# Five edits to one long kernel: the norms' root on columns, the pool layer's copies on ScalarE, an earlier context load, and work moved ahead of three waits

## The chip, the cores and the metric

The kernel runs on one core of one Trainium2 chip. The metric is device time in microseconds for one execution, as the median of several runs. The engines of the core are TensorE (PE, with its weight loads as PEld), VectorE (DVE), ScalarE (ACT), GpSimd (POOL) and SyncE (SP), which mostly issues DMAs.

## The reference, cut to what matters

Two transformer-like blocks follow each other on 512 tokens of 1024 features, all in float32. Every sub-layer begins with the same norm over the features:

```python
def rmsnorm(x, g):
    xf = x.astype(jnp.float32)
    y = xf * lax.rsqrt(jnp.mean(xf * xf, axis=-1, keepdims=True) + EPS)
    return (y * g.astype(jnp.float32)).astype(x.dtype)
```

The first block has four layers: mixers Hyena, windowed attention, pooling and Hyena, each followed by a SwiGLU feed-forward, so eight norms. The pooling mixer takes, for four groups of 256 features, the mean over windows of 3, 5, 9 and 17 tokens, subtracts the input, multiplies each group by a 256x256 matrix, adds a bias and scales. The second block takes a condition vector and a context of 256 tokens. Its two norms are modulated, `norm(x) * (1 + scale) + shift`, with scale and shift from the condition. The first modulated norm is applied to the context too. Then come a bidirectional gated delta rule over eight heads in chunks (it needs the inverse of a unit triangular matrix of each chunk), a latent attention over eight heads, a gated merge of both, and a squared-ReLU MLP.

## The kernel before, in words

All activations lie transposed, feature on partition and token on the free axis. `x` and `xn` are 8 tiles of 128x512. Each engine has one hand-written program, and the engines meet through semaphores. `schedule` gives the stages; each engine has a handler for each stage (`norm`, `hyena`, `attention`, `pool_mixer`, `ffn`, `mod`, `modulate`, `decays`, `gdn`, `mla`, `merge`, `mlp`) and runs them in order. All weights come as one stream of blocks through a ring of four slots. SP issues the loads, and a slot comes free when a named semaphore has a named value. Large products are made in three float32r passes from a high and a low part (L880 to L882 in `split_product`, L891 to L893 in `split_pair`); ACT makes the high part of the weights (L1748) and POOL the low part (L774). PSUM has eight banks: four for `acc` tiles and four for `aux` tiles; in the delta rule they are dealt out as three tables of tiles (`A_AT`, `P_AT`, `R_AT`).

**The norm.** ACT squares the eight tiles of `x` into `xn`, the last one once the last residual tile is there (L1764). DVE folds seven of them into `xn[:, 0]` as they come (L2336). PE multiplies a 128x128 matrix of ones with the folded tile (L867) and with the last square (L870), which leaves the sum over features in every row of one bank. ACT takes the root over 128x512 (L1791), DVE the reciprocal over 128x512 into `rstd` (L2322 in `norm`, L2626 in `modulate`), and then DVE makes the eight tiles of `xn` from `x`, the gain and `rstd` (L2327, or L2628 and L2629). Ahead of a feed-forward each tile is split into a high part on ACT (L1755) and a low part on DVE (L2307); PE starts on the first tile when both are there and goes on tile by tile. There are ten such norms, eight in `norm` and two in `modulate`. The context has its own (L1196 on PE, L2006 on ACT, L2641 on DVE), which the change leaves as it is.

**The pool layer.** DVE does all of it but the products. After the norm it clears two buffers (L2568, L2569), makes the bias column (L2570), and for each of the eight tiles copies `xn` into the padded buffer `xp` (L2575), doubles windows by adding shifted copies (L2578, one to four times), adds, multiplies and subtracts (L2581 to L2583), and adds the bias to `x` (L2584). Then the residual follows. PE's fifth product needs the bank of the first, so it waits for the first residual (L2349).

**The context load.** In stage `mod`, after the last feed-forward, ACT waits for its last product, issues two DMAs (tables, L1994, and the context into `work`, L1995), waits for both, and only then goes into `modulate`, whose first work are the last two squares of the norm.

**The delta rule.** `gdn` on PE runs eleven steps `t`. A step projects head `t` (`proj`, L1314, in pieces of two or four products, set between other work), forms the products of head `t-1` (`products`), and runs the recurrence of head `t-2` (`lows`, `fills`, `flips` on 32- and 64-wide blocks, then `tr`, `sn`, `ks`, `outs`), each of which waits for ACT or DVE to have emptied the one before. The triangular blocks of 32 are solved by POOL; SP writes them out, waits, and reads them back in another layout; PE waits for them on `blocks_in` ahead of the first `lows` (L1352). At t = 9 and after, the pieces named `q`, `z`, `k` and so on stand for the latent attention's down projections (`TAIL`, L1295); there `q` is a tile of sums whose bank ACT and DVE empty after the last solved blocks are written out.

**The latent attention.** `mla` on DVE ends its set-up with `maxima(0)`, the row maxima of the first unit of scores, after the last pair's `mod_sums`, `heads` and `mod_out`. ACT's `exps(0)` needs them, and it is what empties the two banks that PE's `scores(2)` (L1611, L1612) writes. PE makes `scores(0)` and `scores(1)` first of all, then the last pair's broadcast rows (L1553), a rotation (L1602) and two groups of modulation sums (L1185).

## Time and profile before

| | |
|---|---|
| median of 3 runs | 4485.65 us (4485.53 to 4496.6) |
| the profiled execution's own time | 4489.94 us |
| its span, first to last instruction | 4488.1 us |
| PE busy (matmul), DVE, POOL, ACT | 93%, 47%, 32%, 27% of the span |
| mean granted TensorE clock | 0.956 of full speed |

PE bounds nearly everything, but the busy share of a matmul counts its pipeline too, and it counts a matmul at half the clock as work. A reader looks for stretches in which PE stands still or has its clock halved. In the timeline, a row gives start, length, engine, line, operation, tiles and shapes, how many instructions were merged, and in brackets the idle time of the engine before it with what ended it. A float32 matmul is recorded as two. The granted clock in the windows view is 1.00 at full speed (2.4 GHz) and 0.50 at half (1.2 GHz).

### The profile page before, as it was taken

The page shows a single profiled execution, that of the slowest core. Times are in us where ns is not written, and L with a number is a line of the kernel's source. Part 1 is how long each engine was busy: PE and PEld are TensorE (multiplying, and loading weights), DVE is VectorE, ACT ScalarE, POOL GpSimd, SP SyncE. Part 2 cuts the span into 40 slices and gives each one's busy share as a digit, 9 for nine tenths or more (in the row PEclk, how much of TensorE's full clock was granted, in tenths as well). Part 3 has the DMA queues.
Part 4 walks back from the last instruction along what each step waited for, and adds up shares of the span by engine and source line. Part 5 has one row for each costly group of instructions (what it writes and reads, how often), then busy time and mean ns, then how long its engine had stood idle before and what let it go on. Part 6 is the DMA issues. An engine that isn't in the chain of part 4 may idle for free.

```text
span 4488.1 us, 47580 instructions
## 1 busy us (share of the span) xinstructions
PE 4152.2 (93%) x18926; PEld 3071.3 (68%) x18926; DVE 2123.1 (47%) x3109; ACT 1223.2 (27%) x1709; POOL 1444.5 (32%) x834
## 2 busy tenths in 40 slices
PE   7999999899999599989999998979998999998999
PEld 5656788556788378877557886656666665684887
DVE  6567323365413641375763334456664347404322
ACT  3322222134222121233233222322222224422221
POOL 3311344200344144434023442266564000241443
PEclk9999999999999899999999998989999879999999
DMA  6200232210232123221002221221112112221232
GB/s 179 75 18 21 110 102 88 104 47 29 98 114 83 61 97 115 82 78 63 29 29 103 98 95 60 69 57 33 56 34 57 58 67 66 68 98 64 86 104 78
DMA packets 96910, 333.71 MB, mean 74 GB/s; under 512 B 44337, under 2 KB 47537, under 8 KB 67889
## 3 DMA queue, kind: packets, MB, share of 16 engines
q1 hardware_dynamic: 87968, 311.85, 20.5%
q10 hardware_dynamic: 8720, 18.82, 1.7%
q8 instruction: 151, 2.47, 0.2%
q14 instruction: 71, 0.57, 0.0%
HBM read 317.53 MB, written 13.11 MB: 74 GB/s over the span
## 4 chain that ended last, share of the span: by engine, by line
PE 79%; DVE 14%; POOL 2%; ACT 2%; issue 1%; DMA 1%; SPq 0%; DVEq 0%; ACTq 0%; POOLq 0%
PE bank L880 16%; PE bank L881 16%; PE bank L882 16%; PE bank L1314 5%; PE bank L859 5%; PE bank L1082 3%; PE bank L1032 1%; PE bank L1056 1%; PE bank L1612 1%; PE bank L1611 1%; PE bank L1633 1%; PE bank L1543 1%; DVE xn L2327 1%; POOL tab L761 1%; POOL tab L759 1%
## 5 line engine op out<-in xcount | busy, mean ns | idle before, releaser
L774 POOL TENSOR_TENSOR w_lo<-ring,w_hi 128x2048 fp32r<-128x2048 f32 (+2 forms) x200 | 775.3, 3877 | 1532.7 <-ACT w_hi L1748 1532.7
L880 PE MATMUL bank<-x_hi,w_hi 128*128 128x512 f32 x1584 | 618.3, 390 | 9.7 <-POOL w_lo L774 9.7
L881 PE MATMUL bank<-x_lo,w_hi 128*128 128x512 f32 x1584 | 617.0, 389 | 0.0
L882 PE MATMUL bank<-x_hi,w_lo 128*128 128x512 f32 x1584 | 616.9, 389 | 0.0
L1748 ACT ACTIVATE w_hi<-ring 128x2048 fp32r<-128x2048 f32 (+2 forms) x200 | 322.0, 1610 | 866.9 <-PE bank L882 865.9
L880 PE MATMUL bank<-h_hi,w_hi 128*128 128x512 f32 x960 | 373.9, 389 | 0.4
L881 PE MATMUL bank<-h_lo,w_hi 128*128 128x512 f32 x960 | 373.5, 389 | 0.0
L882 PE MATMUL bank<-h_hi,w_lo 128*128 128x512 f32 x960 | 373.4, 389 | 0.0
L880 PEld LDWEIGHTS bank<-x_hi,w_hi 128*128 128x128 f32 x1584 | 297.7, 188 | 73.4 <-POOL w_lo L774 11.8
L882 PEld LDWEIGHTS bank<-x_hi,w_lo 128*128 128x128 f32 x1584 | 297.8, 188 | 61.9
L881 PEld LDWEIGHTS bank<-x_lo,w_hi 128*128 128x128 f32 x1584 | 297.8, 188 | 61.6
L2363 DVE TENSOR_TENSOR xn<-bank,xn 128x512 f32<-128x512 f32 x88 | 60.8, 691 | 589.0 <-PE bank L882 570.0
L1314 PE MATMUL bank<-xn,ring 128*128 128x512 f32 x496 | 240.0, 621 | 1.4 <-DVE work L2671 1.4
L1082 PE MATMUL bank<-work,tab 128*128 128x512 f32 x512 | 228.0, 603 | 12.5 <-ACT work L1886 11.5
L787 POOL TENSOR_TENSOR ring_r<-ring,merge_hi 128x2048 fp32r<-128x2048 f32 x16 | 73.3, 4584 | 506.8 <-ACT merge_hi L2213 506.8
L2353 DVE TENSOR_TENSOR x<-bank,x 128x512 f32<-128x512 f32 x72 | 49.8, 692 | 393.8 <-PE bank L882 347.3
L880 PEld LDWEIGHTS bank<-h_hi,w_hi 128*128 128x128 f32 x960 | 180.2, 188 | 39.3 <-DVE h_lo L2313 2.1
L882 PEld LDWEIGHTS bank<-h_hi,w_lo 128*128 128x128 f32 x960 | 180.2, 188 | 37.4
L881 PEld LDWEIGHTS bank<-h_lo,w_hi 128*128 128x128 f32 x960 | 180.2, 188 | 37.3
L1082 PEld LDWEIGHTS bank<-work,tab 128*128 128x128 f32 x512 | 97.8, 193 | 133.4 <-issue 126.9
L810 POOL TENSOR_TENSOR work<-work,ring 128x1024 f32<-128x1024 f32 x32 | 77.0, 2429 | 266.4 <-ACT work L1855 266.4
L761 POOL TENSOR_TENSOR tab<-tab 56x31 f32<-56x31 f32 (+15 forms) x248 | 150.7, 608 | 19.4
(457 smaller groups left out, 7394.4 us busy)
## 6 DMA issues: line engine op xcount, KB each, us to landing
ring<-stream SPq DMA_DIRECT2D x212, 1024.0 KB, 4.8
ring<-stream SPq DMA_DIRECT2D x64, 704.0 KB, 4.1
ring<-stream SPq DMA_DIRECT2D x36, 512.0 KB, 3.6
xn<-first_mods SPq DMA_DIRECT2D x8, 1024.0 KB, 6.9
ring<-stream SPq DMA_DIRECT2D x4, 1088.0 KB, 5.0
bias_rows<-work ACTq DMA_DIRECT2D x1, 4096.0 KB, 46.3
work<-bias_rows ACTq DMA_DIRECT2D x1, 3072.0 KB, 11.3
tab<-tabs ACTq DMA_DIRECT2D x1, 2624.0 KB, 16.7
```

The lines of the kernel that those rows point to most:

```text
L761: solve(tt(W[:, 0:i, i:SUB], W[:, 0:i, i:SUB], part, ALU.subtract))
L774: nc.gpsimd.tensor_tensor(w_lo[:, j % 2, 0:cols], ring[:, k % RING, 0:cols], w_hi[:, j % 2, 0:cols], ALU.subtract).then_inc(wlo_set, 1)
L787: nc.gpsimd.tensor_tensor(ring_r[:, w, 0:2 * DT * P], ring[:, w, 0:2 * DT * P], merge_whi[j % 2][:], ALU.subtract).then_inc(wlo_set, 1)
L810: nc.gpsimd.tensor_tensor(pair, pair, decay[:, pq:pq + 1, :].broadcast_to([P, 2, 512]), ALU.mult).then_inc(filt_set, 1)
L859: ins = mm(b[:], w[:, at + k, :], rhs[k] if isinstance(rhs, list) else rhs[:, k, :], start=(k == 0), stop=(k == kt - 1))
L880: mm(b[:], hi[:, at + k, :], rhs_hi, start=(k == 0), stop=False)
L881: mm(b[:], hi[:, at + k, :], rhs_lo[:, k, :], start=False, stop=False)
L882: ins = mm(b[:], lo[:, at + k, :], rhs_hi, start=False, stop=(k == kt - 1))
L1082: ins = mm(b[:], fwd[kind][:, p, q, ft * P:(ft + 1) * P], source(kind)[:, 2 * p + q, :], start=(q == 0), stop=(q == 1))
L1314: ins = mm(b[:, 0:TC] if ctx else b[:], w[:, at + k, :], src[:, k, :], start=(k == 0), stop=(k == DT - 1))
L1748: signal(go(w_hi[:, j % 2, 0:cols], ring[:, k % RING, 0:cols], ACT.Copy), whi_set)
L2363: drain(tt_(h_tmp[:, f % 2, :], bank(t)[:], gate_tmp[:, f % 2, :], ALU.mult), t)
```

## The change

Five edits, in the order of the schedule.

1. **Root on columns.** PE uses the squares as the stationary operand and a column of ones as the moving one, in four matmuls for the folded tile and four for the last square. This gives 128x4 sums twice. DVE copies the first and adds the second into `rstd_col`, ACT takes the root of 128x4, DVE the reciprocal of 128x4, and PE spreads it with four matmuls (a broadcast column as stationary operand, the identity as moving) over a second `aux` bank. DVE's eight products read that bank in the place of `rstd`. A small memset after them frees the bank.
2. **Pool layer.** `xp` has two halves. ACT copies each `xn` tile into one and adds the bias to `x`. DVE's memsets and the bias column go into that layer's norm, ahead of the wait for the sums.
3. **Context load.** ACT issues both DMAs at the start of the last feed-forward. The context lies in `tab` and no longer in `work`. The wait stands in `modulate`, ahead of the context's squares.
4. **Projections ahead of `blocks_in`.** At t = 2 and t = 9 PE does the second half of `z` and all of `k` ahead of the wait. The later calls for these pieces do nothing.
5. **`maxima(0)`** on DVE stands between the last pair's `norm_columns` and its `mod_sums`.

```diff
         one_col = small_t[:, 7:8]
+        rstd_col = small_t[:, 28:32]

...
         hc, o_gdn, gates = carve((DT, TC), (DT, T), (8, UNITS * GH))
-        ctx_raw = carve((1, HOLD), (DT, TC))[1]
+        ctx_raw = tab[:, NTAB2:NTAB2 + DT * TC].rearrange("p (a b) -> p a b", a=DT)

...
         KSEQ, KCTX = slice(TC, MK), slice(0, TC)
-        (xp, sums, dpool) = carve((1, T + 2 * PAD), (2, T + 2 * PAD), (DT, T))
+        (xp, sums, dpool) = carve((2, T + 2 * PAD), (2, T + 2 * PAD), (DT, T))

...
                 pe.wait_ge(folded_set, n["fold"])
-                mm(b[:], ones[:], xn[:, 0, :], start=True, stop=False)
+                for c in range(NB):
+                    mm(b[:, c:c + 1], xn[:, 0, P * c:P * (c + 1)], ones[:, 0:1], start=True, stop=True)
                 n["sq"] += DT
                 pe.wait_ge(squares_set, n["sq"])
-                mm(b[:], ones[:], xn[:, DT - 1, :], start=False, stop=True).then_inc(aux_full, 1)
+                for c in range(NB):
+                    ins = mm(b[:, NB + c:NB + c + 1], xn[:, DT - 1, P * c:P * (c + 1)], ones[:, 0:1], start=True, stop=True)
+                ins.then_inc(aux_full, 1)
+                b = open_aux()
+                pe.wait_ge(rstd_set, n["fold"])
+                for c in range(NB):
+                    ins = mm(b[:, P * c:P * (c + 1)], rstd_col[:, c:c + 1].broadcast_to([P, P]), ident[:], start=True, stop=True)
+                ins.then_inc(aux_full, 1)
                 n["xn"] += DT
...
                 def proj(name, h, lo, hi):
-                    if name == "q" and h == 0:
+                    if name == "q" and h == 0 or hi <= made.get((name, h), 0):
                         return
+                    made[name, h] = hi
                     if h >= GH:
...
                     products(mid, 5)
+                    if t in (2, GH + 1):
+                        proj("z", new, 4, 8)
+                        proj("k", new, 0, 8)
                     if live:
...
                 step(go(small_t[:, 26:27], one_col, ACT.Sqrt))
-                t = full(aux, aux_full)
-                signal(go(rstd, bank(t, aux=True)[:], ACT.Sqrt, bias=eps_col, scale=1.0 / D), root_set)
+                t = aux.take()
+                aux.take()
+                act.wait_ge(aux_drained[aux.place(t)], aux.turn(t) + 1)
+                signal(go(rstd_col, rstd_col, ACT.Sqrt, bias=eps_col, scale=1.0 / D), root_set)
                 if split_target(gain) == "hyena":
...
                 aux.n += 2
+                if layer == DEPTH - 1:
+                    act.dma_start(tab[:, 0:NTAB2], tabs2).then_inc(tabs2_in, 16)
+                    act.dma_start(ctx_raw, ctx_in.rearrange("(k p) t -> p k t", p=P)).then_inc(tabs2_in, 16)
                 ends.clear()
...
             def pool_mixer(s):
+                act.wait_ge(pads_set, 2)
+                for m in range(DT):
+                    act.wait_ge(xn_set, n["xn"] + m + 1)
+                    if m >= 2:
+                        act.wait_ge(pooled, m - 1)
+                    signal(go(xp[:, m % 2, PAD:PAD + T], xn[:, m, :], ACT.Copy), xp_set)
+                    signal(go(x[:, m, :], x[:, m, :], ACT.Identity, bias=bs_col[:, m:m + 1]), biased)
                 n["xn"] += DT
                 acc.n += DT

             def mod(_):
-                act.wait_ge(acc_full, acc.n)
-                act.dma_start(tab[:, 0:NTAB2], tabs2).then_inc(tabs2_in, 16)
-                act.dma_start(ctx_raw, ctx_in.rearrange("(k p) t -> p k t", p=P)).then_inc(tabs2_in, 16)
-                act.wait_ge(tabs2_in, 32)
+                pass

             def modulate(which):
                 norm(None, ("mlp", 0) if which else None)
                 n["xn"] += DT
                 if which == 0:
+                    act.wait_ge(tabs2_in, 32)
                     for k in range(DT):
...
                         fold(k)
-                t = aux.take()
-                n["root"] += 1
-                dve.wait_ge(root_set, n["root"])
-                drain(nc.vector.reciprocal(rstd, rstd), t, True)
+                if gain == ("norm_mix", 2 * DT):
+                    nc.vector.memset(sums[:], 0.0)
+                    signal(nc.vector.memset(xp[:], 0.0), pads_set)
+                    signal(tt_(bs_col, V("pl_b", 0, DT), V("pl_scale", 0, DT), ALU.mult), pads_set)
+                t, rows = rstd_rows()
                 n["xn"] += DT
                 target = split_target(gain)
                 to = (x_hi_h, xn_r) if target == "hyena" else (x_hi, x_lo)
                 for k in range(DT):
-                    signal(stt(xn[:, k, :], x[:, k, :], V(gain[0], gain[1] + k), rstd, ALU.mult, ALU.mult),
+                    signal(stt(xn[:, k, :], x[:, k, :], V(gain[0], gain[1] + k), rows, ALU.mult, ALU.mult),
                            plain_set if target else xn_set)
                     if target and k:
                         low(k - 1, *to)
+                rows_read(t)
                 if target:
...
                     n["sq"] += DT
+
+            def rstd_rows():
+                t = full(aux, aux_full)
+                b = bank(t, True)
+                step(nc.vector.tensor_copy(rstd_col, b[:, 0:NB]))
+                ins = tt_(rstd_col, b[:, NB:2 * NB], rstd_col, ALU.add)
+                drain(ins, t, True)
+                n["root"] += 1
+                dve.wait_ge(root_set, n["root"])
+                signal(nc.vector.reciprocal(rstd_col, rstd_col), rstd_set)
+                t = full(aux, aux_full)
+                return t, bank(t, True)[:]
+
+            def rows_read(t):
+                which = aux_drained[t % BANKS]
+                nc.vector.memset(small_t[:, 25:26], 0.0).then_inc(which, 1)
+                dve.wait_ge(which, t // BANKS + 1)

...
                 inv_count = ring[:, blk.place(k), 0:4 * T].rearrange("p (a b) -> p a b", a=4)
-                nc.vector.memset(sums[:], 0.0)
-                step(nc.vector.memset(xp[:], 0.0))
-                step(tt_(bs_col, V("pl_b", 0, DT), V("pl_scale", 0, DT), ALU.mult))
                 W = T + 2 * PAD
                 for m in range(DT):
                     g = m // 2
                     r = POOL_R[g]
-                    step(nc.vector.tensor_copy(xp[:, 0, PAD:PAD + T], xn[:, m, :]))
-                    src, w, side = xp[:, 0, :], 1, 0
+                    dve.wait_ge(xp_set, m + 1)
+                    src, w, side = xp[:, m % 2, :], 1, 0
                     while w < 2 * r:
                         step(tt_(sums[:, side, 0:W - w], src[:, 0:W - w], src[:, w:W], ALU.add))
                         src, w, side = sums[:, side, :], 2 * w, 1 - side
                     dst = sums[:, side, 0:T]
-                    step(tt_(dst, src[:, PAD - r:PAD - r + T], xp[:, 0, PAD + r:PAD + r + T], ALU.add))
+                    step(tt_(dst, src[:, PAD - r:PAD - r + T], xp[:, m % 2, PAD + r:PAD + r + T], ALU.add))
                     step(tt_(dst, dst, inv_count[:, g, :], ALU.mult))
                     signal(tt_(dpool[:, m, :], dst, xn[:, m, :], ALU.subtract), pooled)
-                    step(ts_(x[:, m, :], x[:, m, :], bs_col[:, m:m + 1], None, ALU.add))
                 blk.take()
+                dve.wait_ge(biased, DT)
                 residual(scale_name="pl_scale")
...
                     step(tt_(gm[:, c, :], gm[:, c, :], gain, ALU.mult))
-                t = aux.take()
-                n["root"] += 1
-                dve.wait_ge(root_set, n["root"])
-                drain(nc.vector.reciprocal(rstd, rstd), t, True)
+                t, rows = rstd_rows()
                 for k in range(DT):
-                    step(stt(xn[:, k, :], x[:, k, :], gm[:, 0, k:k + 1], rstd, ALU.mult, ALU.mult))
+                    step(stt(xn[:, k, :], x[:, k, :], gm[:, 0, k:k + 1], rows, ALU.mult, ALU.mult))
                     signal(ts_(xn[:, k, :], xn[:, k, :], modv[:, shift + k, 0:1], None, ALU.add), plain_set if which else xn_set)
                     if which and k:
                         low(k - 1)
+                rows_read(t)
                 if which:
...
                     norm_columns(p)
+                    if p == PAIRS - 1:
+                        maxima(0)
                     mod_sums(2 * p + 1)
                     heads(p)
                     mod_out(2 * p)
                     mod_out(2 * p + 1)
-                maxima(0)
                 for k in range(MLA_UNITS):
```

Left out: the declarations of four semaphores, the counts of `aux` tiles, which go up by one for each norm on SP and POOL, and the dictionary `made`.

## Rows read from the trace of the kernel before

**Rows 1.** The page, part 4: the chain that ended last, by engine.
```profile
PE 79%; DVE 14%; POOL 2%; ACT 2%; issue 1%; DMA 1%; SPq 0%; DVEq 0%; ACTq 0%; POOLq 0%
```

**Rows 2.** The waits view of TensorE: line, releaser, us in total, times, longest.
```profile
PE bank L867 <- DVE xn L2336: 38.6, 10, 15.8
```

**Rows 3.** Timeline of one norm: start us, us, instruction, [idle before, releaser].
```profile
472.98 0.69 DVE L2336 TENSOR_TENSOR xn<-xn 128x512 f32<-128x512 f32 x1
473.81 1.10 PE L867 MATMUL bank<-xn,ones 128*128 128x512 f32 x2 [1.73 <-DVE xn L2336]
474.75 1.02 PE L870 MATMUL bank<-xn,ones 128*128 128x512 f32 x2
476.66 3.35 DVE L2322 RECIPROCAL rstd_t<-rstd_t 128x512 f32<-128x512 f32 x1 [2.99 <-ACT rstd_t L1791]
480.05 1.54 DVE L2327 SCALAR_TENSOR_TENSOR xn<-x,vec,rstd_t 128x512 f32<-128x512 f32 x2
```

**Rows 4.** Timeline, three stretches: column sums, small operations and broadcasts.
```profile
2855.23 2.29 PE L1412 MATMUL bank<-ones,work 128*128 128x1 f32 x20
2861.37 2.50 PE L1423 MATMUL bank<-ident,tab 128*128 128x128 f32 x20 [0.31 <-DVE tab L2887]
2862.63 0.69 DVE L2895 TENSOR_TENSOR work<-work,bank 128x512 f32<-128x512 f32 x1 [1.32 <-PE bank L1423]
...
3441.32 0.18 DVE L2884 RECIPROCAL tab<-tab 128x4 f32<-128x4 f32 x1
...
3658.35 0.17 DVE L2930 SCALAR_TENSOR_TENSOR tab<-bank,tab 128x8 f32<-128x8 f32 x1 [15.89 <-PE bank L1543]
3658.81 0.22 ACT L2159 ACTIVATE tab<-tab 128x20 f32<-128x20 f32 x1 [9.71 <-DVE tab L2932]
```

**Rows 5.** Timeline of the pool layer: the memsets and the first tile.
```profile
1515.86 0.94 DVE L2568 MEMSET work<- 128x1056 f32 x1 [0.38 <-DVE xn L2327]
1516.86 0.50 DVE L2569 MEMSET work<- 128x528 f32 x1
...
1517.59 0.43 DVE L2575 COPY work<-xn 128x512 f32<-128x512 f32 x1
...
1520.97 0.49 DVE L2584 TENSOR_SCALAR x<-x,small_t 128x512 f32<-128x512 f32 x1
```

**Rows 6.** Timeline from the last feed-forward's end into the modulated norm.
```profile
2767.49 0.69 DVE L2353 TENSOR_TENSOR x<-bank,x 128x512 f32<-128x512 f32 x1 [6.06 <-PE bank L882]
...
2774.98 1.29 ACT L1764 ACTIVATE xn<-x 128x512 f32<-128x512 f32 x2 [19.72 <-DMA work<-ctx_in]
...
2784.57 0.75 DVE L2628 SCALAR_TENSOR_TENSOR xn<-x,gm,rstd_t 128x512 f32<-128x512 f32 x1
```

**Rows 7.** Timeline of the delta rule; last, the windows view of L1314 alone.
```profile
2948.09 2.20 PE L1352 MATMUL bank<-work 32*32 32x32 f32 x48 [17.13 <-DMA work<-solved_n]
2956.76 1.38 ACT L2101 ACTIVATE work<-bank 32x192 f32<-32x192 f32 x4 [6.04 <-PE bank L1366]
...
3022.60 1.40 PE L1352 MATMUL bank<-work 32*32 32x32 f32 x48
...
3461.15 2.20 PE L1352 MATMUL bank<-work 32*32 32x32 f32 x48 [6.76 <-DMA work<-solved_n]
...
2948.00:2969.30 21.30, 13.34 (x24) 4.57 (x24) 0.85 0.34 114
```

**Rows 8.** Timeline, then windows: PE, PEld, DVE, ACT, POOL busy, PEclk, DMA.
```profile
3680.41 1.15 DVE L2957 TENSOR_REDUCE tab<-bank 128x1 f32<-128x512 f32 x2
...
3684.18 2.04 PE L1611 MATMUL bank<-work 128*128 128x512 f32 x2 [6.63 <-ACT tab L2165]
...
3676.00:3680.00 4.00, 1.32 (x9) 0.94 (x8) 3.78 (x7) 0.00 (x0) 0.00 (x0) 1.00 0.00 0
...
3700.00:3702.00 2.00, 2.00 (x11) 2.00 (x11) 0.00 (x0) 1.69 (x5) 0.00 (x0) 0.50 0.00 0
...
2906.40:2908.40 2.00, 2.00 (x5) 0.99 (x6) 1.96 (x2) 1.55 (x2) 1.84 (x3) 0.58 0.00 0
```

More of the change, by code:

```diff
@@ L597, in norm @@
             def norm(_):
-                n["aux"] += 1
+                n["aux"] += 2
                 n["xn"] += DT
@@ L634, in modulate @@
             def modulate(which):
-                n["aux"] += 1 if which else 2
+                n["aux"] += 2 if which else 3
             def decays(_):
@@ L822, in _ @@
             nothing = count(0)
-            run({"norm": count(1), "hyena": hyena,
+            run({"norm": count(2), "hyena": hyena,
                  "attention": passes(12 + 16 * 5, 88), "pool": passes(0, DT), "ffn": split("ffn", FT + 2 * DT), "mod": nothing,
-                 "modulate": lambda which: n.update(aux=n["aux"] + (1 if which else 2)), "decays": count(2),
+                 "modulate": lambda which: n.update(aux=n["aux"] + (2 if which else 3)), "decays": count(2),
                  "gdn": gdn, "mla": nothing, "merge": merge,
@@ L1257, in gdn @@
                 until = TB2("until").rearrange("p (d i) -> p d i", d=2)
-                head_w, opened = {(0, 0): first_w[0]}, {}
+                head_w, opened, made = {(0, 0): first_w[0]}, {}, {}
                 def a_tile(*name):
```

4 lines of the change are left out of this document (added).

## The prediction

> **What bounds the kernel now.** I read the chain that ended last first: it is 79% TensorE and 14% VectorE [rows 1]. So most of the span is matmuls that this change doesn't touch, and what can be won lies where PE stands still with DVE, or a DMA, in its place. The waits view says where: the longest sum is the one ahead of the norm's sum of squares, 38.6 us in ten waits with one of 15.8 [rows 2]. The timeline of those places then gives the chain step by step [rows 3, 5, 6], and of the three waits that the last two edits address [rows 7, 8]. The reader is to see there single-engine chains, with nothing beside them, so a microsecond off the chain is a microsecond off the time, unless something else is late next.
>
> **Norm, ten times.** Now: the last fold ends at 472.98 + 0.69 = 473.67; two products with ones end at 474.75 + 1.02 = 475.77, ACT's root takes until 476.66, DVE's reciprocal over 512 columns 3.35, and the first product with the gain begins at 480.05 [rows 3]. That is 6.38 us. After: PE starts 0.14 later as now [rows 3]; eight column matmuls are 16 records, at 2.29 for 20 [rows 4] 1.85; on DVE a copy and an addition at 0.17 each, the root 0.22, the reciprocal of 128x4 0.18 [rows 4], 0.74 together; four hops between engines and one gap at about 0.1, 0.5; and the broadcast, from the start of the first matmul to DVE's first read, 2862.63 - 2861.37 = 1.26 [rows 4]. Sum 0.14 + 1.85 + 0.74 + 0.5 + 1.26 = 4.49, a gain of 1.9 each. The reciprocal was nearly all of it. Everything behind (x_hi, x_lo, the second block's high weights on ACT and low on POOL) starts from DVE's first products and moves with them, so nothing else becomes late. The memset that frees the bank is of the order of 0.1 and stands behind all eight products; only the last low part waits for it, and PE, which restarts at half clock, is then behind DVE. The unknown is the clock at the broadcast. PE does little from the last dense matmul on, and columns count as little: after a group of 20 the clock stood at 0.58 [rows 8]. If it has fallen by then, the four matmuls and their latency take up to twice 1.26, about 1.0 more. That gives 0.9 to 1.9 a norm; I take the fall in 4 cases of 10, so 1.5. Nine norms are 13.5 (8 to 17); the tenth is below. The clock at the restart of the dense work is half in both versions, so no gain is counted for it.
>
> The Trainium skill, page VectorE: DVE Perf Modes, section on the TRN2 errata, speaks against this edit: operations on SBUF pay a fixed cost each, and it advises tiles of 512 elements or more, so one wide operation should be better than several of four columns. It gives about 150 cycles at 0.96 GHz, by which the three small DVE operations would cost an estimated 0.47 us against 0.52 by the rows; the sum would be the same within 1 us for all ten norms. The rule holds for copies, not against a reciprocal that costs 3.35 for 512 columns and 0.18 for four [rows 3, 4].
>
> **Pool layer.** From each of eight tiles DVE loses a copy of 0.43 and a bias of 0.49 [rows 5] with a gap of 0.03 each: 7.8. Ahead of them go two memsets, 0.94 and 0.50, a small multiplication and the gaps, 1.7 [rows 5], less 0.1 for the new memset. Together 9.5. ACT does the same on its own time: it has the place of one tile (at least 2.9 us: four additions or multiplications at 0.7) for about 1.4 of work, and idles there now. The memsets (the second one is twice as long now) are some 2.1 us while PE makes its column sums, 2.0: hidden, or 0.1 late. Without ACT's cover each tile would wait about 0.8. Range 8.5 to 9.7.
>
> **Context load.** ACT's two last squares are made at 2774.98, after 19.72 idle and released by the DMA, though the last residual ended at 2767.49 + 0.69 = 2768.18 [rows 6]. Without it the last square and fold follow at once, and the fold ends at 2768.9, as it does 0.7 after the residual in other norms [rows 3]. With the new chain the first modulated product begins at 2768.9 + 4.5 = 2773.4 where it now begins at 2784.57 [rows 6]: 11.2. This holds the old chain's sums at half clock, too, which now come at full. Less 0.4 for the broadcast's clock: 10.8 (10 to 11.3). DVE's four small operations for the gain are done during the sums. The two issues on ACT at the start of the last feed-forward cost under 1 us, ahead of work of ACT that waits for PE. The DMAs are 1.9 MB on queues that take a 1 MB block in 4.8 us (the page's part 6) while the ring is blocks ahead: nothing, or a few microseconds once if a block is late.
>
> **Projections ahead of the blocks.** At t = 2 PE waits 17.13 and at t = 9 6.76 [rows 7]. The pieces moved ahead are 24 records of L1314, 13.34 in the stretch that follows, partly at half clock; 10.3 at full. So at t = 2 they fit into the wait. But they were the filler: between `lows` and the first `ks` PE waits six times for ACT or DVE to empty a bank (the longest, four copies, 1.38 [rows 7]), and these round trips of 0.5 to 1.5 us, 3 to 9 in all, now lie bare. At full clock t = 2 gains some 6, and is capped anyway: blocks of the next head are there not much before 3016, and its `lows` start at 3022.60 [rows 7], so 6.7 is the most. But the stretch is then all small matmuls at a clock that the wait has halved, and I expect it to stay at 1.2 GHz until the next dense product: 4 us lost on the small ones, 2 on the dense ones behind. That leaves 0.5 to 1, between -1 and 6.5. At t = 9 the pieces take longer than the wait (3.4, then a wait for the bank of the sums, then 6.9), so `lows` begin at about 3465 and not at 3461.15 [rows 7]; 3.5 gained at full clock, -1.5 if the clock falls in the small ones. I take 1.5 for both together (-3 to 10).
>
> **Maxima.** `scores(2)` waits 6.63 until 3684.18 for ACT's exponentials [rows 8], which wait for DVE's first maxima at 3680.41 [rows 8]. Moved, these come when `scores(0)` is done, some 15 us earlier, and DVE's modulation sums (4 us) behind them are still ready before the broadcast rows. So the whole 6.6 goes. More follows. The clock was 1.00 at 3676 to 3680, and it is 0.50 up to 3702 [rows 8]: the wait halves it, and PE's 17.6 us of work from 3684.2 on run at 1.2 GHz. At 2.4 GHz they take half, 8.8; DVE's second maxima and probabilities then come about 2 too late for the first transposes and give 1 to 2 of it back. Bounds 6.6 and 14; I take 12, as the loop behind it holds the full clock.
>
> The Trainium skill, page TensorE: Matmul & The Clock Gate, section HAM oscillation, says that idle gaps throttle the array again and the work behind each gap starts cold. Here the trace agrees: 1.00 before the wait, 0.50 behind it.
>
> **Sum.** 13.5 + 10.8 + 9.5 + 1.5 + 12 = 47.3. The profiled execution took 4489.94 (span 4488.1), so it would become 4442.6; it lies 4.3 over the median of the runs, which becomes 4485.65 - 47.3 = 4438.
>
> **Rivals.** (a) The gains come short: the broadcast at half clock in every norm (9 x 0.9 = 8.1), 10.3 for the modulated norm, 9 for the pool layer, -3 for the projections, since their filler is gone, and 6.6 for the maxima: 31, 4455. For it speaks that PE's activity is thin in each of these places. (b) The clock is kind: 17 + 11.2 + 9.6 + 10 + 14 = 62, 4424. For it speak small matmuls of 128 columns elsewhere at full clock; against it the 32-wide blocks. (c) Slower: the one-column matmuls of the norms hold the clock down in the dense work behind them. One such group was followed by 0.58 in the next window [rows 8]. If each of nine norms left PE at half clock for 20 us more than now, that costs 10 each: 90 - 47 = 43 slower, 4528. It decides from 47.3 x 2 / 9 = 10.5 us more per norm. Against it: the loss after that group was a matter of 3 to 4 us, which is also what a restart costs now. (d) The change doesn't do what it says: the steps between engines in norm and pool layer take 0.5 and not 0.1, and the norms (13.5) and half of the pool layer (5) bring nothing: 29, 4457, much as (a).
>
> **Chances.** Forecast (39 to 56 gained, 4430 to 4447) 0.55; (a) and (d) 0.22; (b) 0.14; (c) 0.05 slower and 0.04 in a weaker form that ends near no change. A difference under 0.3% (13.5 us) is about what a measurement of this kernel cannot tell from none. Faster 0.91, same 0.04, slower 0.05. The range takes in (a), (b) and (d) up to their values: 4421 to 4458.
>
> **What would show it.** In each norm the first product with the gain 4.4 to 5.5 us after the last fold (above 6: the norm is wrong); in the pool layer no DVE copy and tiles 0.98 shorter; the last fold 0.7 after the last residual of the last feed-forward; at t = 2 a wait near 7 in the place of 17.13, and the distance from `lows` to `ks` 14 to 19 in the place of 21.2; no wait ahead of `scores(2)`, and the clock at 1.00 until the loop. The prediction is wrong if that clock is at half all the same (6 lost), or if dense work behind the norms shows half clock for over 5 us.

## The result and the profile after

| | before | after |
|---|---|---|
| median of 4 runs | 4485.59 us | 4454.32 us |
| lowest to highest | 4485.04 to 4496.6 | 4452.26 to 4461.71 |
| profiled execution, span | 4489.94, 4488.1 | 4452.26, 4450.5 |
| mean granted clock | 0.956 | 0.956 |

The ratio is 0.9927 with a 95% interval of 0.9913 to 0.9940. So the change saves 31 us, where 47 were predicted. The forecast itself (39 to 56 us less, 4430 to 4447) was missed. The sign held, and so did the wide range of 4421 to 4458, which takes in the rivals; the size is that of rival (a).

The page of the kernel after. Part 1 gives busy time, share and instructions of each engine, part 4 the chain that ended last, which answers to [rows 1]:

```profile
PE 4174.7 (94%) x19126; PEld 3110.0 (70%) x19126; DVE 2094.2 (47%) x3123; ACT 1229.7 (28%) x1725; POOL 1442.8 (32%) x834
...
PE 81%; DVE 13%; ACT 2%; POOL 2%; issue 2%; DMA 0%; SPq 0%; DVEq 0%; ACTq 0%; POOLq 0%
```

TensorE's share of the chain rose from 79% to 81%, DVE's fell from 14% to 13% and the DMA's from 1% to 0%. The waits view of TensorE in the kernel after (line, releaser, us, times, longest) has more to say:

```profile
PE bank L873 <- DVE xn L2365: 31.5, 10, 15.9
...
PE bank L904 <- DVE x_lo L2334: 14.6, 8, 3.6
PE bank L882 <- DVE small_t L2380: 13.1, 10, 1.6
...
PE bank L1366 <- DMA work<-solved_n: 4.2, 1, 4.2
PE bank L1641 <- DVE tab L3007: 4.0, 2, 2.1
```

L873 is the old L867, down from the 38.6 of [rows 2]: the 7.1 us went with the context load (ahead of the modulated norm's sums PE now waits 1.67 us, before 9.16). L882 is new, ten waits of PE inside the root on columns. L1641, transposes of the attention loop, waits 2.1 us once, and that wait is new: it comes a few us behind the place from which the wait of 6.63 us [rows 8] went.

**One norm**, the same as in [rows 3], in the timeline of the kernel after, and then the granted clock around it (windows view; the columns are length, then busy time of PE, PEld, DVE, ACT and POOL, then PEclk, DMA share and GB/s):

```profile
471.05 0.69 DVE L2365 TENSOR_TENSOR xn<-xn 128x512 f32<-128x512 f32 x1
...
471.89 1.02 PE L873 MATMUL bank<-ones,xn 128*128 128x1 f32 x8 [1.73 <-DVE xn L2365]
472.78 1.03 PE L877 MATMUL bank<-ones,xn 128*128 128x1 f32 x8
...
474.37 0.30 ACT L1810 ACTIVATE small_t<-small_t 128x4 f32<-128x4 f32 x1 [1.11 <-DVE small_t L2376]
474.76 0.18 DVE L2380 RECIPROCAL small_t<-small_t 128x4 f32<-128x4 f32 x1 [0.49 <-ACT small_t L1810]
475.09 2.05 PE L882 MATMUL bank<-ident,small_t 128*128 128x128 f32 x8 [1.28 <-DVE small_t L2380]
477.25 1.53 DVE L2355 SCALAR_TENSOR_TENSOR xn<-x,vec,bank 128x512 f32<-128x512 f32 x2 [2.30 <-PE bank L882]
...
479.66 0.76 PE L904 MATMUL bank<-x_hi,w_hi 128*128 128x512 f32 x1 [2.52 <-DVE x_lo L2334]
```

```profile
472.00:474.00 2.00, 1.81 (x16) 1.72 (x16) 0.09 (x1) 1.25 (x2) 0.00 (x0) 1.00 0.95 401
474.00:476.00 2.00, 0.91 (x4) 0.94 (x5) 0.41 (x3) 0.30 (x1) 0.00 (x0) 0.64 0.14 57
476.00:478.00 2.00, 1.14 (x6) 0.84 (x4) 0.75 (x1) 0.00 (x0) 0.00 (x0) 0.50 0.00 0
...
484.00:486.00 2.00, 2.00 (x8) 1.59 (x7) 1.90 (x4) 0.67 (x2) 0.00 (x0) 0.80 0.00 0
```

The fold ends at 471.74 and the first product with the gain begins at 477.25: 5.51 us, where it was 6.38. The long reciprocal is gone (0.18), but the clock falls between 474 and 476 and the spread (L882, the four matmuls that turn the column into rows) runs at 1.2 GHz, 2.05 us for eight records. The dense products restart at 479.66 and the clock stays at half into the window of 484. In the kernel before they restarted at 482.46, and the window with the rise is this one:

```profile
486.00:488.00 2.00, 2.00 (x9) 1.63 (x8) 1.90 (x4) 0.90 (x2) 0.00 (x0) 0.83 0.00 0
```

**Context and attention.** The timeline at the last feed-forward's end and in the modulated norm, and the attention's loop start, in the kernel after:

```profile
2748.45 0.69 DVE L2399 TENSOR_TENSOR x<-bank,x 128x512 f32<-128x512 f32 x1 [6.06 <-PE bank L895]
2749.18 0.69 DVE L2365 TENSOR_TENSOR xn<-xn 128x512 f32<-128x512 f32 x1
...
2755.88 0.75 DVE L2668 SCALAR_TENSOR_TENSOR xn<-x,gm,bank 128x512 f32<-128x512 f32 x1 [2.30 <-PE bank L882]
...
2920.05 2.20 PE L1366 MATMUL bank<-work 32*32 32x32 f32 x48 [4.18 <-DMA work<-solved_n]
2938.96 1.23 PE L1388 MATMUL bank<-work 128*128 128x128 f32 x4 [0.77 <-DVE work L2827]
...
2994.14 1.40 PE L1366 MATMUL bank<-work 32*32 32x32 f32 x48
...
3653.47 1.54 PE L1641 MATMUL bank<-ident,tab 128*128 128x128 f32 x6 [2.08 <-DVE tab L3007]
```

The last fold follows the last residual at once and ends at 2749.87, 0.73 us after it. Its wait on the DMA, 19.72 us of ACT's time in [rows 6], is gone.

**A table of stages.** Single times of this kernel scatter by some 15 us, so I compare stretches of the trace. For each kernel below I took from the timeline the end of the last fold and the start of the first gain product of all ten norms (as 471.74 and 477.25 above). "Norms" is the sum of the ten distances between them. The other columns are the distances from a first product to the next norm's last fold: the four feed-forwards together; windowed attention; pool layer; from the first modulated norm to the second, with the delta rule, the latent attention and the merge in it; and the MLP, up to the end of its last residual. The two Hyena layers stand apart. The 15 to 16 us ahead of the first norm's last fold and the 8 us behind the last residual are left out.

| us | norms | 4 FF | attention | pool | delta rule to merge | MLP | all of these | two Hyenas |
|---|---|---|---|---|---|---|---|---|
| before | 67.2 | 1478.4 | 276.0 | 59.7 | 1320.9 | 368.6 | 3570.9 | 894.0 |
| after | 59.3 | 1472.4 | 276.9 | 50.2 | 1313.1 | 368.3 | 3540.3 | 886.8 |
| after, second trace (run 5) | 57.5 | 1472.5 | 276.6 | 50.2 | 1313.7 | 368.4 | 3539.0 | 896.8 |
| 1 norm only | 58.4 | 1481.0 | 276.7 | 60.3 | 1319.6 | 369.4 | 3565.3 | 907.2 |
| 2 pool only | 67.6 | 1478.4 | 276.1 | 49.7 | 1324.1 | 368.6 | 3564.5 | 900.6 |
| 3 context only | 65.6 | 1470.6 | 276.0 | 59.7 | 1320.2 | 368.6 | 3560.7 | 903.6 |
| 4 maxima only | 67.1 | 1478.4 | 276.1 | 59.7 | 1311.5 | 368.6 | 3561.4 | 897.2 |
| 8 projections only | 67.4 | 1478.1 | 276.0 | 59.7 | 1324.2 | 367.1 | 3572.4 | 892.3 |
| 7 fillers ahead | 54.6 | 1474.2 | 277.1 | 50.5 | 1311.4 | 368.4 | 3536.0 | 906.8 |
| 6 fillers all around | 52.9 | 1468.5 | 277.8 | 50.7 | 1312.3 | 368.3 | 3530.6 | 886.4 |
| 9 without t = 9 | 59.1 | 1472.5 | 276.9 | 50.3 | 1310.1 | 369.7 | 3538.7 | 884.5 |
| 10 ... fillers behind | 59.5 | 1470.4 | 275.3 | 50.6 | 1315.1 | 368.3 | 3539.1 | 897.9 |
| 11 ... fillers all around | 53.1 | 1468.5 | 277.8 | 50.6 | 1308.8 | 368.4 | 3527.2 | 895.9 |
| 12 ... old root, fillers | 65.3 | 1469.4 | 276.3 | 50.4 | 1313.7 | 367.0 | 3542.1 | 885.0 |

The Hyena layers hold most of the scatter: no kernel changes their work, and their sum goes from 884.5 to 907.2, with more or fewer stretches at half clock. What is left repeats within 1.3 us between the two traces of the changed kernel, and says -30.6 and -31.9 us, the same as the medians. Two limits: a Hyena layer, too, begins behind a norm, so what a norm's edit does to its start is not in this sum; and the stretch between the modulated norms scatters by some 4 us where nothing in it was changed (1320.9, 1324.1 and 1320.2 before and in runs 2 and 3).

### The profile page after: what moved, and what is told of

It reads as the page before. It is cut to its first block, busy times and chain, and to the rows that moved or that the text cites. A ratio compares the mean times of both kernels' runs of the same rounds, so it can differ in the third digit from the quotient of the medians.

```text
span 4450.5 us, 48055 instructions
## 1 busy us (share of the span) xinstructions
PE 4174.7 (94%) x19126; PEld 3110.0 (70%) x19126; DVE 2094.2 (47%) x3123; ACT 1229.7 (28%) x1725; POOL 1442.8 (32%) x834
## 4 chain that ended last, share of the span: by engine, by line
PE 81%; DVE 13%; ACT 2%; POOL 2%; issue 2%; DMA 0%; SPq 0%; DVEq 0%; ACTq 0%; POOLq 0%
PE bank L893 16%; PE bank L894 16%; PE bank L895 16%; PE bank L1328 5%; PE bank L864 5%; PE bank L1095 2%; PE bank L1045 2%; PE bank L1069 1%; PE bank L1308 1%; PE bank L1629 1%; PE bank L1628 1%; PE bank L1650 1%; PE bank L1560 1%; DVE xn L2355 1%; PE bank L1589 1%
## 5 line engine op out<-in xcount | busy, mean ns | idle before, releaser
L894 PEld LDWEIGHTS bank<-x_lo,w_hi 128*128 128x128 f32 x1584 | 297.7, 188 | 61.6
```

The costliest lines, as they stand in the source:

```text
L894: mm(b[:], hi[:, at + k, :], rhs_lo[:, k, :], start=False, stop=False)
```

## The experiments

All were timed in five rounds against the kernel before on their chip, whose median there was 4493.3 (runs 1 to 4), 4490.0 (5 to 8) and 4490.7 us (9 to 12).

### Runs 1 to 4 and 8: each edit alone

Each is the kernel before with one numbered edit of the change; the diffs are those shown above.

> The kernel before with the root on columns alone. The prediction's own step gives 13.5 us less (9 norms at 1.5). The theory from the trace of the changed kernel: the first product comes only 0.87 us earlier (5.51 against 6.38 us behind the last fold), since the spreading matmuls run at half the clock (2.05 us for eight rows), and about half of that is lost again because the dense products that restart earlier stay at half the clock longer: 0.4 us a norm, so 3 to 5 us less in all, with last fold to first product at 5.5 us.

Measured: 4494.57 us, ratio 0.9999 (0.9986 to 1.0011). Last fold to first product is 5.50 us at the same norm as above. The ten distances fell by 8.8 us, but behind the norms the four feed-forwards are 2.6 longer, attention 0.7, pool layer 0.6, MLP 0.8: 4.7 of the 8.8 are given back. All but the Hyenas: 5.5 us less, 1.4 of it between the modulated norms, which the edit hardly touches, so some 4 are the norms'; and the Hyenas of this trace took 13 more. The whole runs allow a gain of 6.3 us at most (ratio 0.9986), so the term of 13.5 is refuted; my lower figure of 3 to 5 fits the trace, and the whole runs can't tell it from nothing.

> The kernel before with the pool layer's edits alone. The prediction's step gives 9.5 us less, and so does the shift between the two traces over that stage (2.5 us ahead of it, 12.5 behind it, 0.5 of it the norm's). Rival: ScalarE's copies are late for the first tiles or collide with VectorE's adds, then under 8 us.

Measured: 4486.77 us, ratio 0.9989 (0.9979 to 0.9998). The pool layer's stretch is 10.0 us shorter (59.7 to 49.7). The total outside the Hyenas fell by 6.4 only, because the stretch between the modulated norms, which the edit doesn't touch, came out 3.2 longer in this trace.

> The kernel before with the early context load alone. The prediction's step gives 10.8 us less in this stage. The trace of the changed kernel: last fold 7.5 us earlier against the dense end and the first modulated product 2.2 us nearer to it, of which the root on columns has 0.9, so 8.8 us less; if the load's traffic in the last feed-forward costs the weight stream anything, less still.

Measured: 4480.84 us, ratio 0.9971 (0.9959 to 0.9982). The last feed-forward's stretch is 7.5 us shorter and the modulated norm 1.8 (8.17 to 6.38): 9.3 us. With the load in it the last feed-forward takes 367.0 us, as the first two do (366.9 and 366.8), so the load costs the weight stream nothing that can be seen.

> The kernel before with the first maxima moved alone. The prediction's step gives 12 us less, with the clock at 1.00 from the last broadcast rows into the loop. The trace of the changed kernel gives 7 us: the wait of 6.6 us ahead of scores(2) is gone, but a wait of 2.1 us ahead of the first transposes stands in its place, and the clock falls to half for 13.7 us there where it was 20.5.

Measured: 4484.63 us, ratio 0.9979 (0.9971 to 0.9988); the stretch between the modulated norms is 9.4 us shorter. Here the loop does what the prediction said. Timeline and windows of this kernel:

```profile
3689.95 0.87 PE L1624 MATMUL bank<-ident,tab 128*128 128x128 f32 x6 [2.09 <-DVE tab L2966]
...
3684.00:3688.00 4.00, 3.85 (x12) 1.61 (x12) 3.76 (x8) 0.00 (x0) 0.00 (x0) 1.00 0.00 0
3688.00:3692.00 4.00, 2.05 (x9) 1.20 (x10) 3.62 (x12) 2.75 (x7) 0.00 (x0) 1.00 0.02 4
```

The same wait of 2.09 us as in the kernel after, but the clock holds at 1.00 and the six transposes take 0.87. In the kernel after they take 1.54, behind the same wait:

```profile
3652.00:3654.00 2.00, 0.53 (x3) 0.53 (x4) 1.83 (x6) 1.51 (x4) 0.00 (x0) 0.59 0.00 0
3654.00:3656.00 2.00, 2.00 (x7) 1.15 (x5) 1.79 (x7) 1.26 (x4) 0.00 (x0) 0.50 0.00 0
...
3664.00:3666.00 2.00, 2.00 (x7) 1.19 (x6) 0.78 (x2) 0.74 (x3) 0.00 (x0) 0.50 0.01 4
```

What that is worth can be read from the last group of modulation sums to the last fold of the second modulated norm. The rows are these, of the kernel before, of run 4 and of the kernel after (their place is plain from the line of the sums, L1185 and then L1198):

```profile
3676.98 0.58 PE L1185 MATMUL bank<-ones,work 128*128 128x1 f32 x4 [0.24 <-DVE kbuf L2949]
...
4104.81 0.69 DVE L2336 TENSOR_TENSOR xn<-xn 128x512 f32<-128x512 f32 x1
```

```profile
3684.01 0.58 PE L1185 MATMUL bank<-ones,work 128*128 128x1 f32 x4 [0.35 <-DVE kbuf L2949]
...
4098.77 0.69 DVE L2336 TENSOR_TENSOR xn<-xn 128x512 f32<-128x512 f32 x1
```

```profile
3647.55 0.58 PE L1198 MATMUL bank<-ones,work 128*128 128x1 f32 x4
...
4068.32 0.69 DVE L2365 TENSOR_TENSOR xn<-xn 128x512 f32<-128x512 f32 x1
```

Before it is 427.8 us, in run 4 414.8 and in the kernel after 420.8: against this trace of before the edit is worth 13.0 us where the clock survives the little wait and 7.0 where it doesn't. But the stretch without the edit has two values of its own: 427.8 or 427.9 in three traces (before, runs 2 and 8), where the half clock behind the wait lasts 20.4 us, and 424.3 and 424.5 in runs 1 and 3, where it lasts some 13.7. Against those two the edit is worth 9.6 and 3.6. From that wait to the last fold, run 4 took 409.5 us, and the eight other traces with this edit 415.0 to 415.5. It survived in one of nine. That one is also the only one without the other four edits, so chance and their influence aren't told apart.

> The kernel before with both pulled-ahead projections alone. The prediction's step: 0.5 to 1 us less at t=2, with the wait of 17.1 us ahead of the blocks down to about 7, and between 3.5 less and 1.5 more at t=9, 1.5 less in all. The trace of the changed kernel over the delta rule gives 1.5 less; its parts: 5 us gained ahead of the first solved head, 2 lost again by the next, about 1 lost at t=9.

Measured: 4492.22 us, ratio 1.0008 (0.9999 to 1.0016): nothing, or a loss of a few us. The delta rule's first `lows` don't come earlier: they stand 163.6 us behind the first modulated product, before 163.5, since they wait for the solved blocks either way. The next head's don't come sooner either. The last head's come 3.5 us later (680.1 against 676.6), and what follows them takes 644.0 against 644.4.

### Runs 5 to 7: what takes the clock in the norm

Run 5 is the changed kernel again. Run 6 adds filler matmuls to every norm on PE, run 7 only the first two groups. Nothing of the result depends on them:

```diff
                 b = open_aux()
+                for i in range(6):
+                    mm(b[:, P * (i % NB):P * (i % NB + 1)], ones[:], ident[:], start=True, stop=True)
                 n["fold"] += 1
...
                 b = open_aux()
+                for i in range(4):
+                    mm(b[:, P * (i % NB):P * (i % NB + 1)], ones[:], ident[:], start=True, stop=True)
                 pe.wait_ge(rstd_set, n["fold"])
...
                 ins.then_inc(aux_full, 1)
+                for i in range(9):
+                    mm(sums_b[:, P * (i % NB):P * (i % NB + 1)], ones[:], ident[:], start=True, stop=True)
                 n["xn"] += DT
```

> The changed kernel once more, as the measure for the two runs with filler matmuls beside it: some 31 us less than before, 28 to 38 from run to run, since the two Hyena layers alone came out up to 7 us longer or shorter in the traces seen so far.

Measured: 4459.55 us, ratio 0.9931 (0.9919 to 0.9943).

> The changed kernel with filler matmuls in each norm (ones times the identity, 128 columns each, results overwritten or never read): six ahead of the folded tile, four ahead of the spread, nine behind it. Theory: the clock falls because PE stands still around the root; kept busy it stays at 1.00, the spread takes 1.0 us in place of 2.05, last fold to first product is 4.5 us in place of 5.5, and the dense products restart at full clock, which saves another 2.2 to 2.6 us in the seven norms with products right behind: 20 to 26 us less than the changed kernel. Rival: PE's idle time at the root is not what takes the clock (the fall is set by something else, or fillers of this kind don't hold it); then the half clock stays and the time is the same within 3 us.

Measured: 4448.21 us, ratio 0.9912 (0.9896 to 0.9927): 11 us less than run 5 by the medians, though the intervals of the two ratios overlap, and 8.4 less outside the Hyenas (7.0 if the stretch between the modulated norms, which has no filler in it, is left out too). That is more than the rival allows and half of what my theory asked. The norm in question in the timeline and the windows of run 6:

```profile
468.33 1.05 PE L875 MATMUL bank<-ones,xn 128*128 128x1 f32 x8 [0.30 <-DVE xn L2371]
469.24 1.03 PE L879 MATMUL bank<-ones,xn 128*128 128x1 f32 x8
470.13 1.22 PE L883 MATMUL bank<-ident,ones 128*128 128x128 f32 x8
471.46 2.07 PE L886 MATMUL bank<-ident,small_t 128*128 128x128 f32 x8
473.33 2.73 PE L889 MATMUL bank<-ident,ones 128*128 128x128 f32 x18
```

```profile
468.00:470.00 2.00, 1.70 (x16) 1.67 (x16) 0.27 (x1) 1.76 (x3) 0.00 (x0) 1.00 0.73 307
470.00:472.00 2.00, 1.89 (x13) 1.62 (x13) 0.50 (x3) 0.30 (x1) 0.00 (x0) 0.77 0.40 168
472.00:474.00 2.00, 2.00 (x12) 2.00 (x11) 0.35 (x1) 0.00 (x0) 0.00 (x0) 0.50 0.00 0
474.00:476.00 2.00, 2.00 (x16) 1.86 (x15) 1.89 (x4) 1.26 (x2) 0.00 (x0) 0.88 0.00 0
```

PE stands still for 0.30 us ahead of the column sums and is busy for 1.70 and 1.89 of each two microseconds, and yet the clock falls, right behind sixteen records of one column each, and the spread takes 2.07. Idle time is not what takes it here. The nine fillers behind bring it back before the dense products start (0.88 in the last window), and the first, second and fourth feed-forward are 1.4 us shorter each than in run 5 (366.0 against 367.4). In three of the nine norms for which the trace has the clock it held, and there the spread took 1.16 us, although the same sixteen records stand there and PE was idle for 0.19 to 0.65 us ahead of the spread. So the columns can take the clock, and don't always.

> The same without the nine fillers behind the spread. Theory: the spread runs at full clock (first product 4.5 us behind the last fold, 1 us a norm, 9 us in all), but PE then stands still for 2.5 us and the dense products start partly at half clock: 9 to 18 us less than the changed kernel. Rival: no difference.

Measured: 4468.05 us, ratio 0.9947 (0.9935 to 0.9958); outside the Hyenas 2.9 us less than run 5, and with 10 more in the Hyenas 8.5 more in the median. The norms fell by 2.9, the feed-forwards behind them rose by 1.7: without the fillers behind, what the spread gains is mostly lost at the restart. The 9 to 18 us that I asked of it did not come.

### Runs 9 to 12: one edit less, and the old root kept warm

Runs 9 to 12 pull the projections ahead at t = 2 only:

```diff
-                    if t in (2, GH + 1):
+                    if t in (2,):
```

> The changed kernel with the projections pulled ahead at t=2 only. Theory: at t=9 the pulled-ahead pieces cost 3.4 to 4.2 us (from the first piece of the last solved head to the first maxima the kernel with both projections alone took 215.5 us, the one before 212.1, and over the attention behind it nothing came back), while t=2 gives 2.5 us ahead of the first solved head; so the delta rule's end comes 3 to 4 us earlier than in the changed kernel. Rival: the loss belongs to t=2, whose work moved into the wait is missed as cover later; then this kernel loses nothing and gains nothing against the changed one.

Measured: 4454.9 us, ratio 0.9921 (0.9905 to 0.9936). Between the modulated norms it is 3.0 and 3.6 us under the two traces with t = 9, as expected, but over all traces with this loop the four with t = 9 average 1312.6 (after and runs 5 to 7) and the four without 1311.9 (9 to 12). The heads ahead of t = 9 scatter by more than the effect, so it is better to start at the seventh head's `lows`, which come ahead of the moved pieces. These are the seventh and the eighth head's `lows` in the kernel after, and then in run 9:

```profile
3369.91 1.40 PE L1366 MATMUL bank<-work 32*32 32x32 f32 x48
...
3435.31 1.40 PE L1366 MATMUL bank<-work 32*32 32x32 f32 x48
```

```profile
3367.29 1.40 PE L1366 MATMUL bank<-work 32*32 32x32 f32 x48
...
3429.95 2.20 PE L1366 MATMUL bank<-work 32*32 32x32 f32 x48 [7.49 <-DMA work<-solved_n]
```

The step is 65.4 us in all five traces with t = 9 (after, runs 5 to 8) and 61.6 to 62.7 in the nine without. From the seventh head's `lows` to the last fold it takes 699.1 or 699.2 in the four traces with t = 9 and this loop, and 696.2, 699.1, 695.8 and 696.1 in runs 9 to 12; run 8 has 709.4 where before has 706.3. So t = 9 costs 3 us at its own step, and in three of the four kernels without it the 3 us are still there at the end; only run 10 shows no difference. A gain shows nowhere.

> The same with nine filler matmuls behind each spread and none ahead. Theory: what matters is that PE is busy in the last 2.5 us before the dense products; the spread stays at half clock (first product at 5.5 us), the products start at or near full clock, 1 to 1.5 us a norm, 8 to 11 us in all less than without fillers. Rival: only with the fillers ahead is the clock back in time; then under 4 us.

Measured: 4457.07 us, ratio 0.9926 (0.9912 to 0.9940); outside the Hyenas 0.4 more than run 9. The same three feed-forwards are 0.8 to 1.4 us shorter each, but the norms are not, the third feed-forward is 1.4 longer, and the stretch between the modulated norms 5.0, in which no filler stands. With that stretch left out as well, the three kernels without fillers (after, runs 5 and 9) take 2227.1, 2225.2 and 2228.5 us, run 10 takes 2224.1, run 7 2224.6, and runs 6 and 11 take 2218.3 both. So the rival holds: fillers behind alone are worth some 3 us, those ahead alone some 2, and all of them 7 to 10. The gain takes all three groups.

> The same with six, four and nine fillers, the intended best version. Theory: 11 to 16 us less than without fillers, as between the two kernels of the earlier pair, so some 45 us less than before.

Measured: 4446.63 us, ratio 0.9907 (0.9891 to 0.9923), 8 us less than run 9 and 11.5 less outside the Hyenas (10.2 without the stretch between the modulated norms). By the median this is the fastest version, 42 to 44 us under the kernel before, but its interval overlaps those of runs 6 and 9 and of the change.

> The same four other edits, but with the root over 128 rows as before, six fillers ahead of the folded tile and 24 behind the sums, through the whole root and up to the first product. First product 6.4 us behind the last fold. If matmuls of one column are what takes the clock in the root on columns, it holds 1.00 here through the whole norm, and the kernel is within 5 us of the one with fillers and the root on columns. Rival: PE's clock falls here too in the norms, and it is 10 us or more behind that one.

Here the root is that of the kernel before. The six fillers ahead of the folded tile stay, and behind the sums PE gets 24 in place of thirteen:

```diff
                 mm(b[:], ones[:], xn[:, DT - 1, :], start=False, stop=True).then_inc(aux_full, 1)
+                if aux.n >= BANKS:
+                    pe.wait_ge(aux_drained[aux.place(aux.n)], aux.turn(aux.n))
+                for i in range(24):
+                    mm(bank(aux.n, aux=True)[:, P * (i % NB):P * (i % NB + 1)], ones[:], ident[:], start=True, stop=True)
```

Measured: 4462.88 us, ratio 0.9935 (0.9921 to 0.9949). The windows of run 12 around the same norm, whose last fold ends at 468.72:

```profile
468.00:470.00 2.00, 1.70 (x8) 0.96 (x7) 0.69 (x1) 1.89 (x2) 0.00 (x0) 1.00 0.78 270
470.00:472.00 2.00, 2.00 (x15) 1.59 (x14) 0.35 (x1) 0.91 (x3) 0.00 (x0) 1.00 0.60 254
472.00:474.00 2.00, 2.00 (x20) 2.00 (x20) 2.00 (x1) 0.00 (x0) 0.00 (x0) 1.00 0.00 0
474.00:476.00 2.00, 2.00 (x19) 1.93 (x18) 1.93 (x3) 0.12 (x1) 0.00 (x0) 1.00 0.00 0
```

Two matmuls of 512 columns (four records) stand where run 6 had eight of one column (sixteen records), PE's busy time in the first window is the same 1.70, and the clock never falls. The same read in nine windows, from each last fold to its first product (the trace has no clock for the first norm), gives 1.00 in all nine norms of run 12, and 0.76 to 0.89 in six of the nine of run 6. That is the cleanest pair of this study: with fillers all around, the columns take the clock in six of nine norms and the wide sums in none. Run 11 repeats the six of nine. The pair is not quite pure: run 12 has no spread and no short idle time ahead of one (0.1 to 0.65 us in run 6). My expectation was badly built, though. It set "within 5 us" against "10 or more behind" as if only the clock differed, but the old root is itself 12 us longer over ten norms (65.3 against 53.1). The kernel is 16 us behind run 11 although its clock held everywhere.

## Why the prediction was right and wrong, point by point

The prediction had named two signs of being wrong: a half clock in the attention loop, and dense work behind the norms at half clock for over 5 us. Both came.

- **Norm: the term was mis-sized, 13.5 predicted, 4 to 5 measured.** Over the nine norms the distance fell by 5.7 us in one trace of the changed kernel and 7.2 in the other, and what follows gave 2 back, 3.6 and 5.2 net; run 1 has 4 to 5.5 for all ten. Two steps failed. The chance of the fall ahead of the spread was put at 4 in 10 with a gain of 1.9 otherwise; in each of the nine norms of which the trace has the clock, it fell (in one of them just behind the start of the spread). The gain was 0.5 to 1.1 us in seven of the eight that are left without the first modulated one, with 0.9 as the text's lower bound; in the eighth the clock fell so early that the column sums ran at half as well, and the distance even grew, to 7.12. And "the clock at the restart is half in both versions, so no gain is counted" left out a loss: PE restarts earlier but doesn't get its clock back as much earlier, so it works 5.1 us at half (479.66 to 484.8, by the 0.80 of the window of 484) where it was 4.2 (482.46 to 486.7, by a 0.83 in the window of 486 of the kernel before). The term's range of 8 to 17 didn't hold. The text had the sign for it, "dense work behind the norms at half clock over 5 us", and that is what the trace showed. The other numbers of the chain were good: column sums 1.92 against 1.85, reciprocal 0.18.
- **Pool layer: right.** 9.5 in the changed kernel (59.7 to 50.2), 10.0 alone, 9.5 predicted. There is no copy on DVE in it; ACT's copy takes 0.63 and its bias 0.72, hidden behind each tile.
- **Context: right in kind, 1 us too high.** 10.8 predicted, 9.6 measured (7.4 in the last feed-forward's stretch, 2.2 in the norm), 9.3 alone. The last fold follows the last residual as predicted. What is missing is again the clock: the spread at half, and in this trace the second half of the column sums with it (1.54 us for eight records, where the first eight took 1.02).
- **Projections: 1.5 predicted, nothing gained, some 3 us lost at t = 9.** The steps at t = 2 came much as written: the wait is 4.18 us (predicted near 7), `lows` to `ks` 18.9 us (14 to 19), and, as the prediction expected, the clock stayed at 0.50 behind the first `lows`, until 22 us behind their start, where it was 6 before. The step after shows where it goes. From one head's `lows` to the next the kernel after takes 2994.14 - 2920.05 = 74.1 us, before 3022.60 - 2948.09 = 74.5 [rows 7]. At t = 9 the prediction had 3.5 gained, or 1.5 lost if the clock falls in the small matmuls, and took the gain into its 1.5. The clock did fall there: at 0.50 from 5 to 26 us behind the start of the last `lows` in all five traces with the edit, while without it the half clock ended 5 to 15 us behind them. Run 8, with this edit alone, gave a ratio of 1.0008 (0.9999 to 1.0016).
- **Maxima: 12 predicted, 7.0 measured, 13.0 at best.** These are against the one trace of before; against the shorter of the two values that the stretch has without the edit they are 3.6 and 9.6. The wait of 6.6 us is gone. The clock at 1.00 through the loop came true in one trace of nine, and there the term was about right; in the others a new wait of 2.1 us (the probabilities, behind DVE's `heads`) comes with a half clock in the loop. The prediction named this as what would make it wrong, with 6 lost, and 6.0 are. What it had not seen is the wait that does it.
- **The sum.** 4.4 + 9.5 + 9.6 and 7.5 for projections and maxima together (1320.9 to 1313.4) make 31.0, the two traces say 30.6 and 31.9, the medians 31.3. The forecast leaned to the kinder answer on the clock in norm and maxima, and that is where most of its 16 us went, 9 and 5. Rival (a), which took half clock everywhere, named 31 and was almost exact. Its mechanism was right, but that it met the number is luck: its norms (8.1) were 4 too high, and its -3 for the projections, right for t = 9, was made up by 3.3 us in a stretch that no edit touches: from the latent attention's first column sums (L1543, L1560) to its first modulation sums (L1185, L1198) the kernel after took 37.4 us, before 40.7. Runs 5 to 7 and 11 have 37.4 there as well, and all others 40.7 or 40.8; why is not shown.
- **Rival (c)**, dense work held down for 20 us behind column matmuls, did not come: the dense work ran at half clock for 1 us more, 5.1 against 4.2. That column matmuls can take the clock was real, the size was not. **The median before** repeated: 4485.59 against 4485.65.

The Trainium skill's page TensorE: Matmul & The Clock Gate, section HAM oscillation, puts the fall on idle gaps of PE, longer ones than in the two places that follow. At the loop of the latent attention the granted clock fell in eight traces of nine with only 2.1 us idle. In the norm of run 6 the traces show another way: 0.30 us idle, PE busy, and still 0.50. There the measurement decides.

## What to carry to other kernels

A chain that replaces one wide operation by matmuls of one column and small operations looks short in the timeline, but the matmuls in it must be priced at half clock, with the restart behind them, unless a trace shows them at full. When such a chain stands between dense stretches, cheap filler matmuls of 128 columns all around it are worth trying; here ten norms gave 7 to 10 us in the traces for 19 fillers each, and whole runs barely show it. And where one stretch of a kernel scatters by more than the effect, add up the others from the trace: five edits worth 31 us could be told apart that way, while whole runs could not tell the norms' edit from nothing.

## What the runs showed of the hardware

- One-column matmuls that keep PE busy for 2 us (sixteen records, 1.02 us for each eight) can take the clock to half with 0.30 us of idle time ahead of them (six of nine norms in run 6, and six of nine in run 11); two matmuls of 512 columns in the same place, at the same busy time, did not (none of nine in run 12).
- The same stretch of instructions can keep or lose its clock: behind the wait of 2.1 us in the attention loop it stayed at 1.00 in run 4 and fell to 0.50 in the kernel after and seven more traces, 6 us apart; in the norms of run 6 it held in three of nine. The two Hyena layers, untouched, took 884.5 to 907.2 us in fourteen traces.
- A gain product that reads its row factor from PSUM takes the same 0.77 us (1.53 for two) as from SBUF (1.54 for two).
